# A two-block transformer kernel: one unrolled pipeline of 32 pairs for the last attention

## The reference, cut to what matters

```python
def odd_mixer(h_x, h_c, w_in, w_out, sink, rpb, cos, sin, with_ctx):
    scale = HEAD_DIM ** -0.5
    ...
    o_c = windowed_attend(qc_x, kc_x, vc_x, kc_c, vc_c, sink).reshape(B, T, -1)
    o_d = neighborhood_attend(qd_x, kd_x, vd_x, kd_c, vd_c, rpb)
    out_x = jnp.concatenate([o_c, o_d], axis=-1) @ w_out

def windowed_attend(q, k, v, k_ctx, v_ctx, sink):
    ...
    valid = (jnp.abs(j - C_WINDOW - i) <= C_WINDOW)[None] & (kpos >= 0) & (kpos < T)
    s_loc = jnp.where(valid[None, :, None, None], s_loc, NEG)
    ...
    p = jax.nn.softmax(jnp.concatenate([sk, s_ctx, s_loc], axis=-1), axis=-1)

def neighborhood_attend(q, k, v, k_ctx, v_ctx, rpb):
    ...
    s_loc = jnp.einsum('brqhd,brshd->brhqs', qg, kg).astype(jnp.float32) + bias
    s_loc = jnp.where(col_valid, s_loc, NEG)
    ...
    p = jax.nn.softmax(jnp.concatenate([s_ctx, s_loc], axis=-1), axis=-1)
```

## Time and profile before

| what | value |
|---|---|
| median of 3 runs | 4299.95 us (4299.09 to 4310.45) |
| the profiled execution | 4310.55 us, span 4308.8 us |
| granted TensorE clock, mean | 0.925 |
| busy: TensorE, VectorE, ScalarE, GpSimd | 3881.4, 2204.6, 1664.4, 53.3 us |

### The profile page before, as it was taken

One profiled execution on the slowest core, in us unless ns is written; L12 is line 12 of the kernel. 1 busy time (PEld: TensorE's weight loads), 2 busy tenths in 40 slices (PEclk: granted clock), 3 DMA queues, 4 the chain that ended last, 5 costly groups with the idle time before them and its releaser, 6 DMA issues.

```text
span 4308.8 us, 52229 instructions
## 1 busy us (share of the span) xinstructions
PE 3881.4 (90%) x18218; PEld 3154.0 (73%) x18218; DVE 2204.6 (51%) x3735; ACT 1664.4 (39%) x2458; POOL 53.3 (1%) x104
## 2 busy tenths in 40 slices
PE   7999979998999988999797867799998888788997
PEld 5888857876878866877586656688887766676885
DVE  4634557777643456778345553523333446545333
ACT  3333444323233354332536654412222346553222
POOL 0000000000000000001000000000000000000000
PEclk9999989998999999999897757999999987789999
DMA  3212313454221322446115000111111110112222
GB/s 120 89 59 88 111 55 117 145 177 135 97 71 58 107 93 78 144 143 214 47 59 51 0 0 15 39 64 64 61 60 49 64 35 0 26 41 69 93 93 73
DMA packets 117857, 334.51 MB, mean 78 GB/s; under 512 B 38127, under 2 KB 38895, under 8 KB 117103
## 3 DMA queue, kind: packets, MB, share of 16 engines
q1 hardware_dynamic: 83087, 269.06, 20.1%
q0 software_dynamic: 14400, 52.44, 3.9%
q10 hardware_dynamic: 20256, 11.53, 1.0%
HBM read 330.89 MB, written 6.97 MB: 78 GB/s over the span
## 4 chain that ended last, share of the span: by engine, by line
PE 78%; DVE 10%; ACT 5%; issue 3%; DVEq 2%; DMA 1%; ACTq 1%; SPq 0%
PE PS L376 12%; PE PS L377 12%; PE PS L378 12%; PE PS L726 10%; PE PS L729 10%; PE PS L727 10%; PE PS L783 3%; PE PS L763 2%; PE PS L757 2%; PE PS L426 2%; PE PS L514 2%; DVE PB L1484 1%; DVE PTL L2005 1%; PE PS L523 1%; ACT PTH L1275 1%
## 5 line engine op out<-in xcount | busy, mean ns | idle before, releaser
L1494 DVE TENSOR_TENSOR WL<-RAW,WH 128x1024 fp32r<-128x1024 f32 x494 | 604.5, 1224 | 544.4 <-ACT WH L937 540.7
L937 ACT ACTIVATE WH<-RAW 128x1024 fp32r<-128x1024 f32 x494 | 521.3, 1055 | 686.6 <-PE PS L729 371.2
L376 PE MATMUL PS<-HHI,WH 128*128 128x512 f32 x1632 | 655.6, 402 | 41.9 <-DVE HLO L1531 36.8
L377 PE MATMUL PS<-HLO,WH 128*128 128x512 f32 x1632 | 646.8, 396 | 0.0
L378 PE MATMUL PS<-HHI,WL 128*128 128x512 f32 x1632 | 641.4, 393 | 0.0
L726 PE MATMUL PS<-H2HI,WH 128*128 128x512 f32 x1472 | 531.2, 361 | 46.6 <-DVE H2LO L1944 35.3
L727 PE MATMUL PS<-H2LO,WH 128*128 128x512 f32 x1472 | 501.1, 356 | 0.0
L729 PE MATMUL PS<-H2HI,WL 128*128 128x512 f32 x1472 | 436.0, 356 | 0.0
L376 PEld LDWEIGHTS PS<-HHI,WH 128*128 128x128 f32 x1632 | 309.5, 190 | 134.4 <-issue 47.1
L726 PEld LDWEIGHTS PS<-H2HI,WH 128*128 128x128 f32 x1472 | 280.1, 190 | 126.2 <-issue 40.9
L378 PEld LDWEIGHTS PS<-HHI,WL 128*128 128x128 f32 x1632 | 309.8, 190 | 70.2
(11 more groups left out here) (281 smaller groups left out, 6404.9 us busy)
## 6 DMA issues: line engine op xcount, KB each, us to landing
RAW<-in_stream SPq DMA_DIRECT2D x494, 512.0 KB, 3.3
MODW<-in_modw POOLq DMA_DIRECT2D x96, 512.0 KB, 4.1
bias_rows<-in_rpb SPq DMA_DIRECT2D x1, 4762.5 KB, 54.2
BIAS<-bias_rows ACTq DMA_DIRECT2D x20, 224.0 KB, 3.9
MEM<-in_mem ACTq DMA_DIRECT2D x3, 1024.0 KB, 4.8
X<-in_x SPq DMA_DIRECT2D x1, 2048.0 KB, 9.1
CROW<-in_crow POOLq DMA_DIRECT2D x4, 512.0 KB, 4.8
out<-X SPq DMA_DIRECT2D x1, 2048.0 KB, 7.4
```

What stands on the lines that cost most here:

```text
L376: nc.tensor.matmul(out, WH[:, slot, b * P:(b + 1) * P], hi, start=start, stop=False)
L377: nc.tensor.matmul(out, WH[:, slot, b * P:(b + 1) * P], lo, start=False, stop=False)
L937: A(WH[:, d, :], RAW[:, s, :], ACT.Copy).then_inc(high_split, 1)
L1494: TT(WL[:, d, :], RAW[:, s, :], WH[:, d, :].bitcast(F32), ALU.subtract).then_inc(split_ready, 1)
```

## The change

The layer's attention no longer runs in `heads`, but in `attention_pairs`, written out for all 32 pairs: chunk j = k // 4, query block k % 4, both halves in one step. The parts:

- scores of both halves alternate, product by product; banks 0 and 1 take half 0, banks 2 and 3 half 1;
- a band pair has only the local key blocks within reach, 2, 3, 3 and 2 of 4, and the two context blocks;
- ScalarE no longer scales probabilities. GpSimd writes the inverse on a diagonal (`DIAG`), and the transposition is a plain product with it;
- the transposed halves have their own places (banks 4 and 5; banks 5 and 6), the values bank 7;
- low parts of queries, keys and values are computed in place on GpSimd (`keep_low`), high parts on ScalarE (`keep`), one item at a time between the pairs; only the first queries and keys are done by VectorE; GpSimd also adds the column mask to the bias;
- queries are scaled by 1/8 when they leave the projection (`take2`), so bias and sink are taken unscaled;
- the first seven eighths of the first output unit stand between the last two pairs' value products.

The blocks of a pair and the places of the transposed halves:

```diff
+        def pair_blocks(k):
+
+            qb = k % 4
+            local = range(max(qb - 1, 0), min(qb + 1, 3) + 1) if in_band(k // 4) else range(4)
+            return list(local) + [4, 5]
...
+            return (4 * T if h == 0 else 5 * T + TC) + b * P
```

GpSimd's program:

```diff
+            for k in range(PAIRS):
+                j, qb = k // 4, k % 4
+                for h in range(2):
+                    pool.wait_ge(pair_inverse, 2 * k + h + 1)
+                    nc.gpsimd.tensor_scalar(DIAG[:, h, :], IDENT[:], MX[:, 4 + h:5 + h], None, ALU.mult).then_inc(pair_diag, 1)
+                if j < 7 and qb == 1:
...
+                    keep_low(U2R[:, Q_CHUNK[j + 1], :], U2[:, Q_CHUNK[j + 1], :], PAIR_QH[j + 1], kept)
+                if 3 <= j < 7 and qb == 2:
...
+                    keep_low(U2R[:, K_CHUNK[j + 1], :], U2[:, K_CHUNK[j + 1], :], PAIR_KH[j + 1], kept)
+                if 3 <= j < 7 and qb == 3:
...
+                    keep_low(U2R[:, V_CHUNK[j + 1], :], U2[:, V_CHUNK[j + 1], :], PAIR_VH[j + 1], kept)
+                if k == 2:
+                    grid_bias(0)
+                if 4 <= j < 7 and qb == 2:
+                    grid_bias(j - 3)
```

TensorE's program:

```diff
+                    if k:
+                        pe.wait_ge(pair_max, 2 * k)
...
+                    for o, k0, k1 in ((0, local[0] * P, (local[-1] + 1) * P), (T, T, TA)):
+                        for x, (lq, rk) in enumerate(((qh, kh), (qh, kl), (ql, kh))):
+                            for h in range(2):
+                                rows = slice(h * HD, h * HD + HD)
+                                last = nc.tensor.matmul(FLAT[:, 2 * h * T + o:2 * h * T + o + k1 - k0], lq[rows, q], rk[rows, k0:k1],
+                                                        start=x == 0, stop=x == 2)
...
+                def turned(k, h):
+
+                    pe.wait_ge(pair_diag, 2 * k + h + 1)
+                    n = len(pair_blocks(k))
+                    ready = 0
+                    for b in list(range(n)) if h == 0 else list(range(2, n)) + [0, 1]:
+                        needed = 2 * k - 1 if h == 0 and b < 4 else 2 * k + 1 if h == 1 and b < 2 else 2 * k
+                        if needed > ready:
+                            pe.wait_ge(pair_low, needed)
+                            ready = needed
+                        at = pair_turned_at(h, b)
+                        last = nc.tensor.matmul(FLAT[:, at:at + P], PAIR_P[k % 2][h][:, b * P:(b + 1) * P], DIAG[:, h, :], start=True, stop=True)
+                    last.then_inc(pair_turned, 1)
...
+                for k in range(-1, PAIRS + 1):
+                    if k + 1 < PAIRS:
+                        scores(k + 1)
+                    if 0 <= k < PAIRS:
+                        turned(k, 0)
+                    if k >= 1:
+                        values(k - 1, 0)
+                    if 0 <= k < PAIRS:
+                        turned(k, 1)
+                    if k >= 1:
+                        values(k - 1, 1)
+                    if k == PAIRS - 1:
+                        between()
```

ScalarE's program, and VectorE's. `exps` is the exponential, `maximum` the bias and maximum, `inverse` the reciprocal, `turned_high` and `turned_low` the high and low part of the transposed probabilities, `out_high` and `out_low` the outputs. `keep` of one item of the next chunk stands behind ScalarE's rows, and `grid_bias` issues four transfers:

```diff
+                for k in range(-1, PAIRS + 1):
+                    j, qb = k // 4, k % 4
+                    if 0 <= k < PAIRS:
+                        turned_high(k, 0)
+                    if k + 1 < PAIRS:
+                        exps(k + 1, 0)
+                    if 0 <= k < PAIRS:
+                        turned_high(k, 1)
+                    if k >= 1:
+                        out_high(k - 1)
+                    if k + 1 < PAIRS:
+                        exps(k + 1, 1)
...
+                    if k == 16:
+                        grid_bias(1)
+                    if k in (19, 23):
+                        grid_bias((k - 19) // 4 + 2)
...
+                for k in range(-1, PAIRS + 1):
+                    if k + 1 < PAIRS:
+                        maximum(k + 1, 0)
+                    if 0 <= k < PAIRS:
+                        turned_low(k, 0)
+                    if k + 1 < PAIRS:
+                        maximum(k + 1, 1)
+                        inverse(k + 1, 0)
+                    if 0 <= k < PAIRS:
+                        turned_low(k, 1)
+                    if k >= 1:
+                        out_low(k - 1)
+                    if k + 1 < PAIRS:
+                        inverse(k + 1, 1)
```

More of the change, by code:

```diff
@@ L742, in heads @@
+            def heads(bufs, full, diff):
                 nq = 6 if full else 4
@@ L889, in _, with first_out, first_unit @@
                     m.add("qks")
-                else:
[L891 to L899, removed]
-                chunks2(KB, H2HI, H2LO, full)
+                    pe.wait_ge(lo_ready, m.at("lo"))
+                    pe.sem_inc(passed, 1)
+                    chunks2(KB, H2HI, H2LO, full)
+                else:
+                    def first_out(k):
+                        if k >= 4:
+                            pe.wait_ge(pair_out_low, 4 * (k + 1))
+                        return products(bank(3 * slot), slot, k, H2HI[:, k, 0:T], H2LO[:, k, 0:T], k == 0, k == KB - 1)
+                    def first_unit():
+                        set_in(slot)
+                        for k in range(KB - 1):
+                            first_out(k)
+                    slot = m.n["units"] % SLOTS
+                    assert slot == 0
+                    pe.wait_ge(split_ready, m.at("units", 1))
+                    attention_pairs(first_unit)
+                    unit_out(first_out(KB - 1))
+                    chunk2(H2HI, H2LO, full)
+                    chunks2(KB - 2, H2HI, H2LO, full)
                 statistics(TA if full else T)
@@ L1288, in heads @@
+            def heads(full, block, following):
                 nq = 6 if full else 4
@@ L1423, in _ @@
                 else:
[L1424 to L1432 removed]
+                    attention_pairs()
                 def of_y2(k, dst, n):
@@ L1990, in negative_max @@
                     dve.sem_inc(passed, 1)
[L1991 removed]
+                    c0 = 2 * h * T
+                    TTR(p[:, 0:n - TC], FLAT[:, c0:c0 + n - TC], added, 1.0, least, ALU.add, ALU.max, MX[:, 0:1])
                     dve.drain()
[L1993 to L1997 removed]
@@ L2006, in transposed_low, with heads @@
                    PTH[:, par, 0:b, q, :].bitcast(F32), ALU.subtract).then_inc(ptl_ready, 1)
-            def heads(bufs, full, block, following, bias=None, sink=None, after_scores=None, behind=None):
+            def heads(bufs, full, block, following):
                 nq = 6 if full else 4
@@ L2014, in maximum @@
                 def maximum(n):
-                    half, qb = n // nq, n % nq
-                    negative_max(n, n_keys(n), bias and bias(half, qb), sink and sink(half), probs(n, 1 if bufs is FIRST else 2, bias is not None))
+                    negative_max(n, n_keys(n))
                 def inverse(n):
@@ L2045, in heads @@
                         maximum(n + 2)
-                        if n + 2 == last and after_scores is not None:
-                            dve.drain().then_inc(after_scores, 1)
                     if n == last - 1:
```

264 lines of the change are left out of this document (172 added, 92 removed).

## The result

The changed kernel takes 4167.16 us (median of 4 runs, 4163.56 to 4169.81) against 4305.20 for the kernel before on the same chip; the ratio is 0.9672, 95% interval 0.9657 to 0.9687, so 3.3% faster. The forecast was 4180. The drop is 138.0 us; 119.6 was forecast, from the earlier median of 4299.95.

What follows compares the result with a forecast made beforehand. TensorE was taken as the bound, through its clock, lost at edges between heads. Filling 5.3, periods 203, low clock 4, tail 9.4, transfers 4 and GpSimd 3 gave 228.7 us, 119.6 less, so 4180; range 4158 to 4225.

Steps and rivals of the forecast that it cites:

- What bounds the kernel now: Block 2's odd-layer attention: TensorE bounds through its clock, lost at drains between heads; 10.7 us a pair, near the slow 11.5.
- Scores on TensorE: Score products of both halves overlap fully: 1.45 us in a grid pair (bounds 1.45 and 2.5), 1.2 in a band pair.
- Rival 1: The halves' score products don't overlap: 21 us more, 4201 us; chance 0.1.
- Transposes: Diagonal products cost 0.224 us against 0.135 for a transpose: 2.7 us a grid pair, 2.0 a band pair.
- The loop that sets the period: Chain through ScalarE, VectorE and TensorE per pair, with 0.2 us added for waits: 6.6 us grid, 6.1 band.
- Ends: Start and finish of the stage: first scores at 3498.8, filling 5.3 us, low clock 4, tail 9.4.
- Queues: Work queued on ScalarE and GpSimd: bias transfers lose 4 us, late diagonals behind K staging and both masks 3 us.
- my sign of no wait over 1 us at a head's end: Expected in the changed profile: no wait over 1 us at a head's end, except behind ScalarE's transfers.
- Rival 2: GpSimd three times VectorE's time or more on masks and staging, diagonals queue: 10 to 25 us, 4190 to 4205; chance 0.1.
- Rival 3: Clock stays at 1.2 GHz: throughout, 4296 us, chance 0.02; band part half the time, 4200 to 4225, chance 0.09.
- Rival 4: GpSimd's diagonals set the period: at 6 us each, about 40 us slower, 4340 us; chance 0.02.
- Rival 5: Tighter: no added 0.2 us a pair, no queue losses, band period 5.5: 4161 us or somewhat below; chance 0.1.

Runs made afterwards that it cites:

- drained: Changed kernel with its pipeline of pairs filled and drained once for each head of four pairs, on all engines: 4236.49 us, ratio 0.9834.
- the four edits: Changed kernel drained at each head, with ScalarE's scaling pass and transposes, all four local blocks in band pairs, halves' scores one after the other: 4286.05 us.
- the scaling pass: Changed kernel with ScalarE scaling probabilities in its own pass and TensorE transposing against the identity, no diagonals made: 4200.91 us, ratio 0.9753.
- the second profiles of both kernels: Changed kernel and kernel before, each run again unedited: 4175.76 us (stage 224.8) and 4315.82 us (stage 350.6).

## Why the prediction was right, and by how much it missed

The mechanism held in the main; the forecast of 119.6 us for the stage compares with 126 to 129. Several terms were off, and some of the misses cancel.

- **What bounds the kernel now** (TensorE, through its clock, lost at edges): shown. Clock 0.77 to 1.00 in the grid part; drained, it falls again, and the four edits together bring 0.75 to 0.78 back. One thing I said of it is not borne out: that it rises only after a long dense stretch. In the changed kernel it first rose at 3493.3, after 7.8 us in which TensorE was busy for 4.88.
- **Scores on TensorE**, 1.45 with full overlap: 1.24 measured in a grid pair. I had counted load and tail of both halves (0.37), where one half's 0.19 is enough, and 3 x 0.35 + 0.37 is 1.42, not 1.45. Rival 1 fell. Its price stays untested, since the halves overlap in part even one after the other; that order costs 0.58 us a grid pair.
- **Transposes**: 0.12 a pass, near the 0.112 of the earlier trace rows. The Trainium skill (Perfetto Trace Analysis, Optimizing Tensor Performance) wants logical transposes done as transposes. The trace agrees that one is cheaper than a diagonal product, 0.135 against about 0.24 us. But with the division left out the exchange was worth 11.7 us of stage, not 30, because the loop through the other engines is next and GpSimd's masks cost more. And keeping the division by a pass on ScalarE costs 31.6 more than the diagonals.
- **The loop that sets the period**: 6.6 and 6.1 forecast, 6.46 and 5.87 measured, 16 x 12.33 = 197.3 instead of 203. In a grid pair TensorE sets the period: its own sum is 6.46 and not 6.3 (scores 1.24, diagonals 2.8, values 2.4, where 1.45, 2.7 and 2.1 stood), and the 0.2 that I added for waits without a row does not exist. I had the loop and TensorE as equal there; in the run without the division the loop shows at about 5.9. In a band pair TensorE waits about 0.6 us for VectorE's low part, so the loop sets the period.
- **Ends**: tail 9.4 us, as forecast (3693.8 to 3703.2). Filling and low clock together took 5.8 (what the sum below leaves) instead of 9.3 us, since the clock was up for good 15 to 16 us after the first scores, not 20, and for about 3.5 us before that. Against that the first scores came 6.9 us after the last take, not 5.4: the shared path of VectorE and GpSimd, which I had missed.
- **Queues**, the terms that were mis-sized. ScalarE's transfers: 4 us forecast, about 0.4 measured (0.2 more in the pair after each of the last two places). In its timeline the issues (3641.40 to 3644.26) start beside the output copies and end as the next diagonal set does (3644.13), so they fill idle time; in the scaling pass, where there is little, they stall it by 1.26 to 2.14 us at each place. GpSimd: diagonals 0.6, staging 1.83, masks 2.11, against 0.7, 1.9 and 2.2 assumed. The three places where staging and both masks meet cost 1.48 each, 4.4, and the first masks, in the first band head, 0.75, where 3 us stood in the sum. So my sign of no wait over 1 us at a head's end failed three times, by 1.4 us each.
- **The sum** from the first score product: 197.3 + 5.8 + 9.4 + 5.2 = 217.7 us, as the trace has it, against 228.7: 5.7 less from the periods, 4 from the transfers, 3.5 from the ends, 2.2 back to GpSimd. So 13.2 us of misses stand one way and 2.2 the other, 11.0 in all. The first scores came 1.5 later than forecast, so the stage shrank by 9.5 us more than the 119.6 forecast (6.2 by the second profiles of both kernels). The whole time fell by 138.0 us, 18.4 more than forecast. What is not in the stage lies in code that the diff does not touch, and its cause is open. That the median came within 13 us of the forecast is partly luck: the median of before, from which I counted, was 4299.95 then and 4305.20 beside the changed kernel.
- **Rivals** 2, 3 and 4 did not happen. Rival 5 (tighter, 4161) came nearest: no added waits and next to no transfer losses, but a band period of 5.87 and not 5.5, and the mask waits.

## What to carry to other kernels

An edge in a software pipeline costs its fill, its drain, and then the clock of what follows: 9.1 us here on average, between heads of 23 to 27 us. Edits that leave the clock at 0.87 to 0.93 when they are undone singly took it to 0.75 to 0.78 when all four were, so undo edits singly and together before you add their worth up.

When one operation replaces another, price the loop with it, not the instruction: here the diagonal product costs more than a transpose and still wins 31.6 us, by taking a pass off ScalarE. And when work moves to an idle engine, look at what queues ahead of its one urgent instruction: two masks apart instead of together brought TensorE from 95% to 98% busy in the grid part.

## What the runs showed of the hardware that was not expected

- VectorE's subtraction with both operands in SBUF took 2.56 instead of 0.96 us beside one on GpSimd (1.94 us), and 0.95 once they were apart. It started 0.19 us after GpSimd's and ended 0.81 us after it, which is within 0.14 us of what waiting for GpSimd's end and then running its 0.95 would give. The Trainium skill states such a lock (SBUF — State Buffer, section SBUF: two separate sides); the trace agrees. Beside GpSimd's later stagings and masks VectorE's subtractions from PSUM, 768 columns wide, kept their 957 ns on average.
- Products of 64 rows on different halves of the array overlap also when six of one half stand ahead of six of the other. The second half's first product then starts 0.01 us after the first half's third, before three products that stand ahead of it in the program (halves one after the other, 3640.34).
- TensorE's pace at full clock and 100% busy differs by 1 to 2% between two programs in code that is the same in both (568 and 574 against 579 and 580 products in 100 us).
